# The causal mask of an attention stage: added in PSUM by VectorE ahead of its maximum, instead of by two small products on TensorE

## The reference, cut to what matters

```python
s_s = jnp.einsum('bqghd,bgqnld->bghqnl', qg, k_sel) * scale
mask_s = (tok <= qpos[None, None, :, None, None]).reshape(B, G, 1, Q_BLK, -1)
p_s = masked_softmax(s_s.reshape(B, G, HPG, Q_BLK, -1), mask_s).reshape(s_s.shape)
...
mask_w = (kpos[None, :] <= qpos[:, None]) & (kpos[None, :] > qpos[:, None] - WINDOW) & (kpos[None, :] >= 0)
s_w = jnp.einsum('bqghd,bkgd->bghqk', qg, kwin) * scale
p_w = masked_softmax(s_w, mask_w)
...
o = gb[..., 0:1] * o_c + gb[..., 1:2] * o_s + gb[..., 2:3] * o_w
```

## Time and profile before

| what | value |
|---|---|
| median of three runs | 1384.77 us |
| time of the profiled execution | 1386.17 us |
| its span | 1384.5 us |
| TensorE busy over the span | 1150.4 us (83%) |
| VectorE, ScalarE, GpSimd busy | 408.4, 218.6, 166.6 us (29%, 16%, 12%) |
| the 32 items (first scores to the end of the block) | 431.2 to 530 us of the span |

### The profile page before, as it was taken

The page is one execution under the profiler, slowest core; times in us unless marked ns, Lnnn a source line. Parts: engine busy times, 40 slices in busy tenths (PEclk is TensorE's granted clock), DMA queues, the critical chain, the costliest instruction groups (busy, mean ns, idle before and its releaser), DMA issues. The chain is left out here.

```text
span 1384.5 us, 16284 instructions
## 1 busy us (share of the span) xinstructions
PE 1150.4 (83%) x6697; PEld 584.4 (42%) x6697; DVE 408.4 (29%) x694; ACT 218.6 (16%) x443; POOL 166.6 (12%) x235
## 2 busy tenths in 40 slices
PE   2699999899997897989899982977777887888780
PEld 0343344444555556979644461322222223222230
DVE  4524437622005444345422335110000001011104
ACT  2101123220003552314100120000000000000002
POOL 1100001133002443223100001010000000000003
PEclk9999999889997997999999985999999999899995
DMA  9512326424414006000082431899999999999985
GB/s 342 203 62 91 121 91 243 156 106 125 145 38 130 1 1 243 11 1 4 1 308 99 204 152 46 369 428 425 429 430 430 431 431 430 430 431 431 431 353 197
DMA packets 61333, 311.68 MB, mean 225 GB/s; under 512 B 6194, under 2 KB 12676, under 8 KB 48728
## 3 DMA queue, kind: packets, MB, share of 16 engines
q1 hardware_dynamic: 49784, 273.79, 49.3%
q0 software_dynamic: 9184, 32.82, 6.2%
q10 hardware_dynamic: 2304, 4.20, 0.8%
HBM read 285.11 MB, written 24.64 MB: 224 GB/s over the span
## 5 line engine op out<-in xcount | busy, mean ns | idle before, releaser
L2295 PE MATMUL ps<-ring,zrT 128*64 128x512 f32 x1024 | 258.7, 664 | 68.5 <-DMA ring<-in_moe_w_gate_dram 31.7
L2295 PEld LDWEIGHTS ps<-ring,zrT 128*64 128x64 f32 x1024 | 83.8, 152 | 231.8 <-issue 203.6
L867 PE MATMUL ps<-ring,uT 128*128 128x512 f32 x384 | 170.2, 600 | 1.2 <-PE ps L867 0.6
L2317 PE MATMUL ps<-ring,mg 128*64 128x512 f32 x512 | 117.9, 614 | 21.8 <-DMA ring<-in_moe_w_down_dram 18.2
L858 PE MATMUL ps<-uT,ring 128*128 128x512 f32 x256 | 115.3, 608 | 1.3 <-ACT uT L293 0.7
L867 PEld LDWEIGHTS ps<-ring,uT 128*128 128x128 f32 x384 | 72.5, 192 | 93.4 <-issue 93.4
L2110 DVE TENSOR_TENSOR zrT<-zrT,ps 128x512 f32<-128x512 f32 x16 | 11.0, 687 | 326.9 <-PE ps L2295 326.9
L1924 ACT ACTIVATE zrT<-ps 128x512 f32<-128x512 f32 x16 | 9.6, 597 | 436.4 <-PE ps L2295 436.4
L858 PEld LDWEIGHTS ps<-uT,ring 128*128 128x128 f32 x256 | 48.9, 194 | 67.2 <-issue 66.1
L2317 PEld LDWEIGHTS ps<-ring,mg 128*64 128x64 f32 x512 | 38.4, 142 | 90.8 <-issue 90.5
L1852 POOL DMA_DIRECT2D y_dram<-zrT x16 | 9.1, 569 | 459.0 <-DVE zrT L2120 459.0
(11 more groups left out here) (355 smaller groups left out, 1320.2 us busy)
## 6 DMA issues: line engine op xcount, KB each, us to landing
ring<-in_moe_w_gate_dram SPq DMA_DIRECT2D x32, 2048.0 KB, 19.1
ring<-in_moe_w_up_dram SPq DMA_DIRECT2D x32, 2048.0 KB, 18.4
ring<-in_moe_w_down_dram SPq DMA_DIRECT2D x32, 2048.0 KB, 20.1
ring<-in_w_ada_dram SPq DMA_DIRECT2D x12, 2048.0 KB, 9.4
ring<-in_w_in_dram SPq DMA_DIRECT2D x9, 2048.0 KB, 12.9
y_dram<-zrT POOLq DMA_DIRECT2D x16, 512.0 KB, 10.5
y_dram<-zeros POOLq DMA_DIRECT2D x1, 7680.0 KB
gates_dram<-gst ACTq DMA_DIRECT2D x16, 256.0 KB, 2.0
```

What stands on the lines that cost most here:

```text
L867: ins = pe.matmul(ps[:, n % 4, :], uT[:, k, P * i:P * i + P], w, start=(k == 0), stop=(k == KD - 1))
L2295: ins = pe.matmul(ps[HALF * r:HALF * r + HALF, "gu".index(kind), :], xgT[:, b % 2, k, HALF * r:HALF * r + HALF], w[r][:, k, :], start=(k = ...
L2317: ins = pe.matmul(ps[HALF * r:HALF * r + HALF, 2 + c, :], hdT[:, j, HALF * r:HALF * r + HALF], w[r][:, j, 512 * c:512 * c + 512], start=(j ...
```

## The change

The mask is no longer multiplied in. VectorE adds the float32 mask, which lies in the table of constants, to the diagonal blocks of both g in PSUM, in one instruction of 2 x 128 elements for each partition, and then takes the maximum. The bfloat16 copies of mask and identity, their semaphore `a_bf` and TensorE's wait for it go. The key product now raises `a_S`.

```diff
-                dve.tensor_copy(causal_bf[:, :], C("causal")).then_inc(a_bf, 1)
-                dve.tensor_copy(ident_bf[:, :], C("ident")).then_inc(a_bf, 1)
...
                     if t < NI:
                         dve.wait_ge(a_S, t + 1)
+                        i = items[t][1]
+                        own = ps[:, 2 * (t % 2):2 * (t % 2) + 2, P * i:P * i + P]
+                        link(dve.tensor_tensor(own, own, C("causal").unsqueeze(1).to_broadcast([P, 2, P]), ALU.add))
                         if t >= 4:
                             dve.wait_ge(a_ex, t - 3)
                         dve.tensor_reduce(mx[:, t % 4, :], ps[:, 2 * (t % 2):2 * (t % 2) + 2, 0:rows_of(t)], AX, ALU.max,
...
-                pe.wait_ge(a_bf, 2)
...
-                        pe.matmul(ps[:, 2 * (t % 2) + g, 0:rows_of(t)], qT[r, j, P * i:P * i + P], kT[r, b, 0:rows_of(t)],
-                                  start=True, stop=False)
-                    for g in range(2):
-                        ins = pe.matmul(ps[:, 2 * (t % 2) + g, P * i:P * i + P], ident_bf[:, :], causal_bf[:, :], start=False,
-                                        stop=True)
+                        ins = pe.matmul(ps[:, 2 * (t % 2) + g, 0:rows_of(t)], qT[r, j, P * i:P * i + P],
+                                        kT[r, b, 0:rows_of(t)], start=True, stop=True)
                     ins.then_inc(a_S, 1)
```

More of the change, by code:

```diff
@@ L907, in build @@
         gseen = alloc(stage2, "gseen", [P, 2, NT, CT])
-        causal_bf = alloc(stage2, "causal_bf", [P, P], BF16)
-        ident_bf = alloc(stage2, "ident_bf", [P, P], BF16)
         ynT = ring_slot(0)[:, 0:CT * T].rearrange("p (j t) -> p j t", j=CT)
-        (a_bf, a_qT, a_q, a_kT, a_k, a_sc, a_dve, a_cad, a_csub, a_cex, a_cp, a_cT, a_cTe, a_S, a_mx, a_ex, a_rc, a_scl, a_TR,
+        (a_qT, a_q, a_kT, a_k, a_sc, a_dve, a_cad, a_csub, a_cex, a_cp, a_cT, a_cTe, a_S, a_mx, a_ex, a_rc, a_scl, a_TR,
          a_evD, a_evA, a_PV, a_o, a_oe) = (
-            sem(f"a_{n}") for n in ("bf qT q kT k sc dve cad csub cex cp cT cTe S mx ex rc scl TR "
+            sem(f"a_{n}") for n in ("qT q kT k sc dve cad csub cex cp cT cTe S mx ex rc scl TR "
                                     "evD evA PV o oe").split())
```

## The result

The changed kernel took 1398.09 us in the median of four runs (1395.52 to 1399.74), the kernel before beside it 1385.01 us (1384.37 to 1386.30): a ratio of 1.0094 (95% interval 1.0081 to 1.0108). Four further runs gave 1397.11 us and 1.0086 (1.0066 to 1.0105). The direction was forecast, the size was not: 12 to 13 us instead of 4.5, outside the range of 1386.0 to 1392.5. The profiled execution of the first four, 1395.52 us, was the shortest of them.

A forecast was written before the change was run, and what follows sets the result against it. Latency chains through VectorE and ScalarE, not TensorE's work, were taken to bound the attention block. Steady groups' 2.8 us and the first group's 1.7 made 4.5 us, so 1389.2 us, 0.3% slower; range 1386.0 to 1392.5 us.

The forecast's parts named there:

- What bounds the block: Attention block: four latency chains per 21.62 us steady group, from scores through VectorE and ScalarE to `turned`; TensorE idles 2.20 us.
- the fourth wait: TensorE's 0.75 us idle ahead of `turned` of turn 15: profile names GpSimd, prediction ScalarE's copy of item 11.
- The price of the addition: VectorE's mask addition ahead of each maximum: 0.41 us, 0.45 from start to start, taken from a same-size row.
- The steady part: Groups two to four of the attention block: 12 chains, each 0.23 us longer, 2.8 us in all.
- The first group: Attention block's first group, VectorE-bound: `turned(1)` late by 1.58 us, 1.7 us in all.
- The clock rival: TensorE, idler, stays at its low clock for one more turn in the first group: about 1.5 us on top; 6%.
- The end: Barrier closing the attention block: every later block waits for it, so the delay arrives in full, with nothing added behind.

The follow-up runs named there:

- run 3: Kernel before, with ScalarE's copy of an odd item put ahead of the exponentials of the same turn: 1377.75 us, ratio 0.9953.
- run 9: Changed kernel with three semaphore increments per item on TensorE and nine idle products in its waits of turns 2 to 7: 1390.97 us, ratio 1.0049.
- run 1: Kernel before, with its mask products kept and VectorE's mask addition made as well: 1394.84 us, ratio 1.0074.
- run 2: Changed kernel without the addition, so that the mask is left out altogether: 1385.43 us, ratio 1.0001.
- run 7: Changed kernel padded with four semaphore increments on TensorE behind each item's scores, 128 in all: 1391.49 us, ratio 1.0044.
- run 6: Changed kernel with the zeros written in turn 8 of GpSimd's loop in the attention block, from their own buffer: 1393.53 us, ratio 1.0057.
- run 5: Kernel before, with the zeros written in turn 8 of GpSimd's loop in the attention block, from their own buffer: 1384.93 us, ratio 0.9993.
- run 11: Kernel before, with ScalarE's copies ahead of its exponentials and VectorE's ahead of the maximum from turn 8 on: 1381.37 us, ratio 0.9971.

## Why the prediction was wrong, point by point

**What bounds the block: right.** The four latency chains per group and their releaser, ScalarE's copy behind the exponentials, were read from the timeline; run 3 removes the copy from the chain and the waits go. The row that put the fourth wait down to GpSimd was rightly overruled.

**The price of the addition: right.** 0.43 us and 0.47 with its link, where 0.41 and 0.45 were taken. A write of VectorE to PSUM costs at most 0.02 us more than one to SBUF here. The difference of the two access costs that the Trainium skill gives (Perfetto Trace Analysis, Optimizing Scalar/DVE Operations) would have made it, by estimate, some 0.065 us more; the measured row decides.

**The steady part: right in mechanism, 0.1 us a group too small.** 4 x 0.26 = 1.04 us in the second and third steady groups (the last 0.98, with the block's tail), 0.92 predicted.

**The first group: mis-sized.** It cost 2.8 us where 1.7 stood. `turned(1)` came 14.25 us behind the first scores instead of 12.60, +1.65 for the forecast 1.58, and the transposes of turn 7 +2.01 for 1.7. The row that carries the rest is TensorE's, in the changed kernel:

```profile
455.11 1.39 PE L1076 MATMUL ps<-cst,prob 128*128 128x128 f32 x6 [1.11 <-ACT early L1028]
```

It took 0.88 us before: TensorE's clock had fallen again, which it had not before, and its work up to the scores of turn 8 cost 0.78 us more. The windows of this stretch, in the kernel before and in the changed one (the granted clock is the third number from the end):

```profile
447.00:456.00 9.00, 7.13 (x66) 4.37 (x62) 3.12 (x8) 4.57 (x14) 3.69 (x6) 1.00 0.01 2
455.00:459.00 4.00, 3.89 (x15) 1.87 (x16) 0.96 (x1) 0.06 (x1) 0.00 (x0) 0.57 0.00 0
```

The same low stretch reached into the second group (1.94 us for the scores at 457.06, 1.13 at 456.01 before) and made 0.8 us there; that part run 9 shows. The clock rival, given 6% and 1.5 us, came true with 1.6 us, half of it in the first group, and one of its signs is there: a granted clock below 1.00 in the second group (0.97). I had read the granted clock of a window that was steady and took it for the ramp.

**The end: this is the step that failed.** The prediction said that every later block waits at the barrier and that the delay "arrives in full"; it looked for something that could give time back, and put what could be added behind the attention block at nothing. The attention block's 6.6 us alone would have made 1391.6 us, inside the range. Every later block runs the same instructions, but TensorE's program ahead of them had become shorter, and one of its fetches, late beside the write of the zeros, now falls where TensorE needs it before it is there. The recurrence block is longer by 3.1 us in the first profile and by 5.5 in the second, with the clock's share in it. Runs 1, 2 and 7 bring it or take it away by TensorE's program, run 6 takes it away by moving the write, and run 5 shows that the move alone gives the kernel before nothing. By medians, of the 12 to 13 us some 5.6 are this (the changed kernel against the padded one) and about 6 the rest, for which the profile has 6.6 us in the attention block. The prediction's reason was not quite so either: it read from the DMA share of 0.09 that no transfer of a later block runs meanwhile, but that is a mean; in the first group it is 0.37, with weights that the merge reads (`in_p_rwkv`, `in_p_nsa`). They are through before 442 us, and no row here shows that they cost anything.

The profile of before did show both ingredients: a transfer share of 1.0 at the head of the recurrence block, and an instruction queue on the same engines. The Trainium skill (Runtime: NRT & Kernel Launch, Instruction fetch mechanics) says that instructions come in blocks of 16 KB, fetched while the current one runs, and that the cost of crossing into the next is mostly hidden. The size agrees with the queue's row (0.02 MB for one fetch), and in run 6 the fetch does come ahead of need; beside this write the cost is not hidden, it is 3.0 us in the middle of dense products.

**What stays open.** The 1.2 us behind the recurrence block: the profiles there lie between 740.3 and 742.3 us, mostly higher without mask products, but not always (742.3 in run 11, which has them). Part of the recurrence block's length: 111.2 to 113.7 us among the profiles without a long gap, with TensorE at the lower level for 14 to 23 us of it; what sets that was not tested. And why the clock falls once more in the changed kernel's first group: its waits are longer, which run 9 does not isolate.

**Which version to keep.** The kernel before with ScalarE's copies first, 1377.75 us, is faster than both by 7 and by 20 us. With that order the masked addition costs 4 us when the fetch gap is padded away (1381.78 against 1377.75), nearly all of it in the first two groups.

## What to carry to other kernels

Before work is moved to an engine with room, follow the waits of the busy engine back: a share of 85% busy still left four latency chains per group, and what is added to a chain costs its length however idle its engine is. The better edit was in the same rows: a copy that stood behind a slower instruction in its queue. And after a change that alters the number of an engine's instructions, compare the untouched blocks too: a gap put down to "issue" in dense code beside a saturating transfer may be a late fetch, as here, and it can be told by the start of the instruction queue's packet, by padding the program or by moving the transfer.

## What the runs showed of the hardware

Instruction fetches share the transfer engines with bulk writes: beside a 7.9 MB write at some 400 GB/s one fetch of 16 KB came 4.5 us later than without it and held TensorE for 3.0 and 3.3 us. In all twelve profiles with such a gap, of 0.2 to 3.3 us, TensorE went on 2.25 to 2.5 us behind the fetch's start, in some of them with the write still running. 128 semaphore increments on TensorE's queue, spread over a block, cost nothing measurable (114.3 us with and without). Behind gaps of 3.0 and 3.3 us TensorE's clock was at the lower level, in one of the two for longer, at a cost of another 1.3 us. VectorE adds in place in PSUM in 0.43 us for 256 elements, where two other rows of that size took 0.41 and 0.42.
